# Feed-forward products of an fp32 transformer kernel: one 512-column and one 256-column matmul, or three of 256 columns summed in PSUM

## The chip, the cores and the metric

The kernel runs on one core of a Trainium2 chip. The metric is the device time of one execution in microseconds (us). The program is one launch; weights come from HBM in 314 transfers while the core computes.

## The reference

Two blocks of two layers each act on 256 tokens of width 1024, all in float32. The first block has, per layer, a feed-forward stage, an attention mixer and a second feed-forward stage; the second block has a mixer and a feed-forward stage. There are six feed-forward stages in all, each with an inner width of 2816. What is computed in one (first block; the second block's takes gate and up from one matrix and normalises the result before it is added):

```python
def rms_norm(x, g):
    xf = x.astype(jnp.float32)
    y = xf * lax.rsqrt(jnp.mean(xf * xf, axis=-1, keepdims=True) + RMS_EPS)
    return (y * g.astype(jnp.float32)).astype(x.dtype)

def swiglu(x, w_gate, w_up, w_down):
    return (jax.nn.silu(x @ w_gate) * (x @ w_up)) @ w_down

h = h + 0.5 * swiglu(rms_norm(h, ffn1_norm[l]), ffn1_w_gate[l], ffn1_w_up[l], ffn1_w_down[l])
```

## The kernel before

**Precision.** Every fp32 operand is split in two fp32r halves, a high one (a rounded copy) and a low one (what the copy lost). A product is taken as high x high, high x low and low x high, summed; low x low is left out. Weights and activations both have such halves: `w_hi`, `w_lo` and `x_hl`, `hid_hl`, `m_hl`, where `hl[:, 0, :]` is the high and `hl[:, 1, :]` the low half of 256 tokens, side by side.

**Feed-forward stage.** The activations lie feature by token, so a weight block of 128 x 128 is the stationary operand and the 256 tokens stream past it. `matmul_pair` (line 450) issues two matmuls for a block: one of the high weights with both halves of the activations, 512 columns into a whole PSUM bank (line 452), and one of the low weights with the high half, 256 columns, added into the first half of that bank (line 453). The bank then holds two partial sums of 256 columns, which VectorE (DVE) has yet to add. A stage has 22 gate and up parts in turn (p = 0 to 21, even ones gate, odd ones up; each of 1024 x 256 weights, so 8 x 2 blocks = 16 pairs) and 12 down parts (8, 8 and 6 blocks deep by 2 wide, four times; 176 pairs). That makes 352 + 176 = 528 pairs in a stage and 3168 in six.

**PSUM.** Part p uses two banks, `pair_banks(p)`, in a rotation of three; TensorE (PE) waits before part p until DVE has taken part p - 3. Chunks of the down product have banks of their own (`down_bank`), and banks 6 and 7 are also used for the row statistics.

**DVE in a stage** (`ffn`, line 1221). For each part `both` (line 1231) adds the two halves of two banks in a `tensor_reduce` into SBUF (`g_tmp` or `u_tmp`) and so frees the banks (`up_free`). For a gate part, `scaled_gate` (line 1237) multiplies by `row_b`, the row factor of the normalisation; ScalarE (ACT) applies Silu (line 913). For an up part, `hidden` (line 1242) multiplies gate and up; ACT makes the high half (line 916), and `hidden_lo` (line 1246) the low half. For each down chunk a `tensor_reduce` (line 1277) adds the halves; then lines 1284 and 1285 scale it and add it to `h`, or, in the last stage of each layer of the second block, a second normalisation follows (`post_norm`, line 1179).

**Weights.** A ring of three slots: SyncE's queue loads a part (line 435) once its slot's low half has been made, ACT makes the high half (line 265) once PE has used the part three before, and DVE makes the low half (line 272); PE waits for that.

**The row factor.** In part 0 the squares' sum goes through PE (line 466), DVE (`token_roots`, line 1173), GpSimd (POOL, a power of -0.5, line 1632) and PE again behind part 1 (`to_rows`, line 473); `row_factor` (line 1177) copies it to `row_b`.

**Order.** Each engine's queue is written out by hand and is in order; semaphores tie them. The mixers have their own helpers, `matmul3` (lines 446 to 448, mostly 512 columns) and `project_out`, whose three matmuls (lines 591 to 593) are

```python
nc.tensor.matmul(mixer_out(c), hs[0], mk[:, 0, :], start=first, stop=False, skip_group_check=True)
nc.tensor.matmul(mixer_out(c), hs[0], mk[:, 1, :], start=False, stop=False, skip_group_check=True)
mm = nc.tensor.matmul(mixer_out(c), hs[1], mk[:, 0, :], start=False, stop=m >= 2 and k == kc - 1, skip_group_check=True)
```

Of the kernel before, what the change touches and what calls it, by code (L numbers as in the profile page):

```python
# [17 lines left out]
P = 128  # L18
# [157 lines left out]
def build(nc, w, out):  # L176

    with ExitStack() as ctx:
# [42 lines left out]
        def sem(name):  # L221
            return ctx.enter_context(nc.semaphore(name))
# [11 lines left out]
        up_free, scaled_ready, silu_ready, hid_ready = sem("up_free"), sem("scaled_ready"), sem("silu_ready"), sem("hid_ready")  # L234
# [53 lines left out]
        def pair_banks(p):  # L288

            return 2 * (p % 3)  # L290
# [159 lines left out]
        def matmul_pair(bank, w_h, w_l, hl, start, stop):  # L450

            nc.tensor.matmul(ps[:, bank, :], w_h, hl.rearrange("p x n -> p (x n)"), start=start, stop=False, skip_group_check=True)  # L452
            return nc.tensor.matmul(ps[:, bank, 0:SEQ], w_l, hl[:, 0, :], start=False, stop=stop, skip_group_check=True)  # L453

        @block.tensor
        def _(pe):
# [20 lines left out]
            def ffn(i0, post_norm):  # L477
                x0 = due("xlo_ready", KC) - KC
                u0 = due("up_free", 2 * STEPS) - 2 * STEPS
                h0 = due("hidlo_ready", STEPS) - STEPS  # L480
                for p in range(2 * STEPS):
                    i = i0 + p
                    part_ready(i)
                    if p >= 3:
                        pe.wait_ge(up_free, u0 + p - 2)
# [16 lines left out]
                for q in range(KC // 2):  # L502
                    if q == 1:
                        pe.wait_ge(up_free, u0 + 2 * STEPS)
# [636 lines left out]
        def _(dve):  # L1141
# [79 lines left out]
            def ffn(s, i0, post_norm_):  # L1221
                def both(dst, p):

                    dve.wait_ge(part_used, i0 + p + 1)
                    b = pair_banks(p)
                    taken = STEPS * FFN_BEFORE[s] + p // 2
                    if taken and p % 2 == 0:
                        dve.wait_ge(hid_ready, taken)
                    elif taken:
                        dve.wait_ge(hidlo_ready, taken)  # L1230
                    return nc.vector.tensor_reduce(dst.rearrange("p (f n) -> p f n", f=2), ps[:, b:b + 2, :].rearrange("p b (x n) -> p b n x", x=2),  # L1231
                                                   AX_X, ALU.add).then_inc(up_free, 1)

                def scaled_gate(j):
                    dve.wait_ge(up_free, 2 * STEPS * FFN_BEFORE[s] + 2 * j + 1)
                    g2 = g_tmp.rearrange("p (f n) -> p f n", f=2)
                    nc.vector.tensor_tensor(g2, g2, row_b.unsqueeze(1).to_broadcast([P, 2, SEQ]), ALU.mult).then_inc(scaled_ready, 1)

                def hidden(j):
                    dve.wait_ge(up_free, 2 * STEPS * FFN_BEFORE[s] + 2 * j + 2)  # L1240
                    dve.wait_ge(silu_ready, due("silu_ready"))
                    nc.vector.tensor_tensor(u_tmp, g_tmp, u_tmp, ALU.mult).then_inc(hid_ready, 1)
# [6 lines left out]
                both(g_tmp, 0)  # L1249
# [3 lines left out]
                both(u_tmp, 1)  # L1253
# [4 lines left out]
                for j in range(1, STEPS):  # L1258
                    both(g_tmp, 2 * j)
                    hidden_lo(j - 1)  # L1260
                    scaled_gate(j)
                    split_lo(dve, i0 + 2 * j + 3)
                    both(u_tmp, 2 * j + 1)
                    hidden(j)
                    split_lo(dve, i0 + 2 * j + 4)
                    if s == 0 and j == 1:
                        rope2_angles()
                hidden_lo(STEPS - 1)

                for q in range(KC // 2):  # L1270
                    split_lo(dve, i0 + 2 * STEPS + 3 * q + 3)
                    split_lo(dve, i0 + 2 * STEPS + 3 * q + 4)
                    for c in (2 * q, 2 * q + 1):
# [3 lines left out]
                        m = nc.vector.tensor_reduce(t, ps[:, b, :].rearrange("p (x n) -> p n x", x=2), AX_X, ALU.add)  # L1277
                        if post_norm_:
                            m.then_inc(h_ready, 1)
# [3 lines left out]
                        step(m)  # L1283
                        step(nc.vector.scalar_tensor_tensor(t, t, 0.5, row_b, ALU.mult, ALU.mult))
# [447 lines left out]
```

## Time and profile before

| what | value |
|---|---|
| three runs | 2043.04, 2043.59, 2054.57 us (median 2043.59) |
| the profiled execution | 2051.39 us, span 2049.6 us |
| mean granted TensorE clock | 0.969 of full speed |
| PE busy, DVE busy, ACT busy | 94%, 68%, 46% of the span |
| HBM read | 324 MB, 159 GB/s over the span |

The span runs from the first to the last instruction of the profiled execution; its own time is 1.8 us more. Busy time of PE counts overlapping matmuls once: a matmul's record is longer than the distance to the next one, since the array takes the next matmul before the last has drained. How fast PE goes is therefore read from the distance between starts. PEld is the load of the stationary operand; every matmul has one of its own.

### The profile page before, as it was taken

To read this page: it belongs to the slowest core of one execution; us is meant where nothing else is said; L and a number is where in the kernel's file an instruction comes from. 1 tells how busy PE (TensorE), PEld (TensorE's weight loads), DVE (VectorE), ACT (ScalarE), POOL (GpSimd) and SP (SyncE) were. 2 spreads that over 40 slices of the span, in tenths; PEclk is the share of its full clock that TensorE was granted. 3 is DMA by queue.
4 is the path that set the end of the run, shared out by engine and by line. 5 is a ranking of instruction groups with operands and counts; after the bars stand their busy time and mean duration, and the time that the engine had idled before them with its cause. 6 is when DMAs were issued, how large, how long until landed. Compare 5 with 4: busy or idle time off the path is not lost.

```text
span 2049.6 us, 26068 instructions
## 1 busy us (share of the span) xinstructions
PE 1935.5 (94%) x10928; PEld 1673.8 (82%) x10928; DVE 1394.5 (68%) x1548; ACT 944.3 (46%) x1154; POOL 151.4 (7%) x124
## 2 busy tenths in 40 slices
PE   7999988999999999799999999989997999989997
PEld 6888866988888888679888878878886878878886
DVE  6876678677678776767876446658765446668764
ACT  5444453444444444525444564544443464544442
POOL 0000640000000007200000001100000001100000
PEclk9999998999999999879999999989998999999998
DMA  7555450355555555304545543324554443424552
GB/s 272 185 175 195 164 181 1 124 191 180 184 191 194 180 177 188 134 1 161 189 176 194 185 166 135 128 103 175 188 188 159 144 171 121 157 103 164 191 184 77
DMA packets 47204, 326.77 MB, mean 159 GB/s; under 512 B 5488, under 2 KB 5488, under 8 KB 10864
## 3 DMA queue, kind: packets, MB, share of 16 engines
q1 hardware_dynamic: 46368, 322.78, 44.0%
q10 hardware_dynamic: 720, 2.33, 0.3%
q8 instruction: 86, 1.41, 0.3%
q14 instruction: 30, 0.25, 0.0%
HBM read 324.04 MB, written 1.05 MB: 159 GB/s over the span
## 4 chain that ended last, share of the span: by engine, by line
PE 76%; issue 9%; DVE 7%; POOL 5%; ACT 3%; DMA 0%; POOLq 0%; SPq 0%; ACTq 0%; DVEq 0%
PE ps L452 31%; PE ps L453 16%; PE ps L446 6%; PE ps L448 6%; PE ps L447 6%; ACT w_hi L265 1%; PE ps L644 1%; DVE w_lo L272 1%; POOL arena L1626 1%; PE ps L591 1%; PE ps L593 1%; PE ps L592 1%; POOL arena L1627 1%; POOL arena L1625 1%; PE ps L613 1%
## 5 line engine op out<-in xcount | busy, mean ns | idle before, releaser
L272 DVE TENSOR_TENSOR w_lo<-raw,w_hi 128x2048 fp32r<-128x2048 f32 (+3 forms) x314 | 705.7, 2251 | 334.1 <-ACT w_hi L265 331.7
L265 ACT CAST w_hi<-raw 128x2048 fp32r<-128x2048 f32 (+3 forms) x314 | 583.7, 1861 | 687.6 <-PE ps L453 431.1
L452 PE MATMUL ps<-x_hl,w_hi 128*128 128x512 f32 x2112 | 746.0, 398 | 33.3 <-DVE x_hl L1157 18.1
L453 PE MATMUL ps<-x_hl,w_lo 128*128 128x256 f32 x2112 | 594.8, 282 | 0.0
L452 PEld LDWEIGHTS ps<-x_hl,w_hi 128*128 128x128 f32 x2112 | 399.5, 189 | 125.7 <-issue 33.9
L453 PEld LDWEIGHTS ps<-x_hl,w_lo 128*128 128x128 f32 x2112 | 402.8, 191 | 0.0
L452 PE MATMUL ps<-hid_hl,w_hi 128*128 128x512 f32 x1056 | 371.0, 394 | 0.0
L446 PE MATMUL ps<-w_hi,x_hl 128*128 128x512 f32 (+3 forms) x744 | 287.7, 387 | 15.2 <-DVE x_hl L1157 8.4
L453 PE MATMUL ps<-hid_hl,w_lo 128*128 128x256 f32 x1056 | 299.1, 283 | 0.0
L447 PE MATMUL ps<-w_lo,x_hl 128*128 128x512 f32 (+3 forms) x744 | 283.6, 381 | 0.0
L448 PE MATMUL ps<-w_hi,x_hl 128*128 128x512 f32 (+3 forms) x744 | 283.5, 381 | 0.0
L1231 DVE TENSOR_REDUCE ffn_tmp<-ps 128x512 f32<-128x1024 f32 x132 | 161.6, 1225 | 124.7 <-PE ps L453 124.0
L452 PEld LDWEIGHTS ps<-hid_hl,w_hi 128*128 128x128 f32 x1056 | 198.4, 188 | 45.4
L453 PEld LDWEIGHTS ps<-hid_hl,w_lo 128*128 128x128 f32 x1056 | 198.9, 188 | 0.0
L446 PEld LDWEIGHTS ps<-w_hi,x_hl 128*128 128x128 f32 x744 | 141.6, 190 | 44.3 <-issue 13.8
L448 PEld LDWEIGHTS ps<-w_hi,x_hl 128*128 128x128 f32 x744 | 141.4, 190 | 26.7
L447 PEld LDWEIGHTS ps<-w_lo,x_hl 128*128 128x128 f32 x744 | 141.6, 190 | 25.0
L1632 POOL TENSOR_TENSOR stat<-stat,const 128x2 f32<-128x2 f32 x14 | 19.9, 1423 | 1538.7 <-DVE stat L1173 1029.7
L881 ACT ACTIVATE x_hl<-h,gains 128x256 fp32r<-128x256 f32 x80 | 38.6, 504 | 105.4 <-DVE h L1285 74.5
L591 PE MATMUL ps<-m_hl,w_hi 128*128 128x256 f32 x256 | 73.0, 285 | 0.0
L593 PE MATMUL ps<-m_hl,w_lo 128*128 128x256 f32 x256 | 72.5, 283 | 0.0
L592 PE MATMUL ps<-m_hl,w_hi 128*128 128x256 f32 x256 | 72.5, 283 | 0.0
(215 smaller groups left out, 1704.3 us busy)
## 6 DMA issues: line engine op xcount, KB each, us to landing
raw<-in_parts SPq DMA_DIRECT2D x282, 1024.0 KB, 4.8
raw<-in_parts SPq DMA_DIRECT2D x24, 768.0 KB, 4.2
raw<-in_parts SPq DMA_DIRECT2D x4, 576.0 KB, 3.8
raw<-in_parts SPq DMA_DIRECT2D x2, 832.0 KB, 4.3
raw<-in_parts SPq DMA_DIRECT2D x2, 704.0 KB, 4.0
const<-in_const ACTq DMA_DIRECT2D x1, 1098.0 KB, 8.6
h<-in_x_t SPq DMA_DIRECT2D x2, 512.0 KB, 5.4
out_h<-h SPq DMA_DIRECT2D x4, 256.0 KB, 2.1
```

Of the source, the lines that this page charges most:

```text
L265: nc.scalar.copy(w_hi[:, i % RING, 0:n_of(i)], raw[:, i % RING, 0:n_of(i)]).then_inc(high_ready, 1)
L272: nc.vector.tensor_tensor(w_lo[:, s, 0:n], raw[:, s, 0:n], w_hi[:, s, 0:n].bitcast(F32), ALU.subtract).then_inc(low_ready, 1)
L446: nc.tensor.matmul(out_, a_hi, b_hi, start=start, stop=False, skip_group_check=True)
L447: nc.tensor.matmul(out_, a_hi, b_lo, start=False, stop=False, skip_group_check=True)
L448: return nc.tensor.matmul(out_, a_lo, b_hi, start=False, stop=stop, skip_group_check=True)
L452: nc.tensor.matmul(ps[:, bank, :], w_h, hl.rearrange("p x n -> p (x n)"), start=start, stop=False, skip_group_check=True)
L453: return nc.tensor.matmul(ps[:, bank, 0:SEQ], w_l, hl[:, 0, :], start=False, stop=stop, skip_group_check=True)
L591: nc.tensor.matmul(mixer_out(c), hs[0], mk[:, 0, :], start=first, stop=False, skip_group_check=True)
L592: nc.tensor.matmul(mixer_out(c), hs[0], mk[:, 1, :], start=False, stop=False, skip_group_check=True)
L593: mm = nc.tensor.matmul(mixer_out(c), hs[1], mk[:, 0, :], start=False, stop=m >= 2 and k == kc - 1, skip_group_check=True)
L881: nc.scalar.activation(x_hi(c), h[:, c, :], ACT.Copy, scale=gains[:, s, c:c + 1]).then_inc(xhi_ready, 1)
L1231: return nc.vector.tensor_reduce(dst.rearrange("p (f n) -> p f n", f=2), ps[:, b:b + 2, :].rearrange("p b (x n) -> p b n x", x=2), AX_X, A ...
```

## The change

The 512-column matmul of `matmul_pair` becomes two of 256 columns with the same high weights, first with the high and then with the low half of the activations, and all three matmuls add into the first 256 columns of the bank. The bank then holds the finished sum. The reductions on DVE go: `scaled_gate` and `hidden` read PSUM themselves, and so does the scaling of the down chunks; with the second normalisation a copy of 256 columns stands in the reduction's place. `up_free` goes: PE now waits before part p for `scaled_ready` (p - 3 a gate part) or `hid_ready` (an up part), and before the second pair of down chunks for the last `hid_ready`.

```diff
 def matmul_pair(bank, w_h, w_l, hl, start, stop):
-    nc.tensor.matmul(ps[:, bank, :], w_h, hl.rearrange("p x n -> p (x n)"), start=start, stop=False, skip_group_check=True)
+    nc.tensor.matmul(ps[:, bank, 0:SEQ], w_h, hl[:, 0, :], start=start, stop=False, skip_group_check=True)
+    nc.tensor.matmul(ps[:, bank, 0:SEQ], w_h, hl[:, 1, :], start=False, stop=False, skip_group_check=True)
     return nc.tensor.matmul(ps[:, bank, 0:SEQ], w_l, hl[:, 0, :], start=False, stop=stop, skip_group_check=True)
...
                 if p >= 3:
-                    pe.wait_ge(up_free, u0 + p - 2)
+                    pe.wait_ge(hid_ready if p % 2 == 0 else scaled_ready, u0 + (p - 3) // 2 + 1)
...
                 if q == 1:
-                    pe.wait_ge(up_free, u0 + 2 * STEPS)
+                    pe.wait_ge(hid_ready, u0 + STEPS)
...
             def scaled_gate(j):
-                dve.wait_ge(up_free, 2 * STEPS * FFN_BEFORE[s] + 2 * j + 1)
-                g2 = g_tmp.rearrange("p (f n) -> p f n", f=2)
-                nc.vector.tensor_tensor(g2, g2, row_b.unsqueeze(1).to_broadcast([P, 2, SEQ]), ALU.mult).then_inc(scaled_ready, 1)
+                dve.wait_ge(part_used, i0 + 2 * j + 1)
+                if j or FFN_BEFORE[s]:
+                    dve.wait_ge(hid_ready, STEPS * FFN_BEFORE[s] + j)
+                b = pair_banks(2 * j)
+                nc.vector.tensor_tensor(g_tmp.rearrange("p (f n) -> p f n", f=2), ps[:, b:b + 2, 0:SEQ],
+                                        row_b.unsqueeze(1).to_broadcast([P, 2, SEQ]), ALU.mult).then_inc(scaled_ready, 1)

             def hidden(j):
-                dve.wait_ge(up_free, 2 * STEPS * FFN_BEFORE[s] + 2 * j + 2)
+                dve.wait_ge(part_used, i0 + 2 * j + 2)
                 dve.wait_ge(silu_ready, due("silu_ready"))
-                nc.vector.tensor_tensor(u_tmp, g_tmp, u_tmp, ALU.mult).then_inc(hid_ready, 1)
+                if j or FFN_BEFORE[s]:
+                    dve.wait_ge(hidlo_ready, STEPS * FFN_BEFORE[s] + j)
+                b = pair_banks(2 * j + 1)
+                nc.vector.tensor_tensor(u_tmp.rearrange("p (f n) -> p f n", f=2), ps[:, b:b + 2, 0:SEQ],
+                                        g_tmp.rearrange("p (f n) -> p f n", f=2), ALU.mult).then_inc(hid_ready, 1)
...
-                    m = nc.vector.tensor_reduce(t, ps[:, b, :].rearrange("p (x n) -> p n x", x=2), AX_X, ALU.add)
                     if post_norm_:
-                        m.then_inc(h_ready, 1)
+                        nc.vector.tensor_copy(t, ps[:, b, 0:SEQ]).then_inc(h_ready, 1)
...
-                    step(m)
-                    step(nc.vector.scalar_tensor_tensor(t, t, 0.5, row_b, ALU.mult, ALU.mult))
+                    step(nc.vector.scalar_tensor_tensor(t, ps[:, b, 0:SEQ], 0.5, row_b, ALU.mult, ALU.mult))
```

PE's queue at the start of part 3 of the first stage, the first part that waits for banks; before:

```order
L452 MATMUL ps<-x_hl,w_hi 128x512
L453 MATMUL ps<-x_hl,w_lo 128x256
L452 MATMUL ps<-x_hl,w_hi 128x512 [waits up_free,low_ready]
L453 MATMUL ps<-x_hl,w_lo 128x256
L452 MATMUL ps<-x_hl,w_hi 128x512
```

and with the change:

```order
L452 MATMUL ps<-x_hl,w_hi 128x256
L453 MATMUL ps<-x_hl,w_hi 128x256
L454 MATMUL ps<-x_hl,w_lo 128x256
L452 MATMUL ps<-x_hl,w_hi 128x256 [waits scaled_ready,low_ready]
L453 MATMUL ps<-x_hl,w_hi 128x256
L454 MATMUL ps<-x_hl,w_lo 128x256
```

Two instructions for a block became three, and the wait is now for the scaled gate of part 0.

DVE's queue at the start of the first stage, from the low half of part 2 to the products of parts 0 and 1; before:

```order
L272 TENSOR_TENSOR w_lo<-raw,w_hi 128x2048 [waits high_ready]
L1231 TENSOR_REDUCE ffn_tmp<-ps 128x512 [waits part_used]
L1173 TENSOR_SCALAR stat<-ps 128x2 [waits sum_done]
L272 TENSOR_TENSOR w_lo<-raw,w_hi 128x2048 [waits high_ready]
L1231 TENSOR_REDUCE ffn_tmp<-ps 128x512 [waits part_used]
L1177 COPY arena<-ps 128x256 [waits bcast_done]
L1237 TENSOR_TENSOR ffn_tmp<-ffn_tmp,arena 128x512 [waits up_free,dve_step]
L272 TENSOR_TENSOR w_lo<-raw,w_hi 128x2048 [waits high_ready]
L1242 TENSOR_TENSOR ffn_tmp<-ffn_tmp 128x512 [waits silu_ready,up_free]
```

and with the change (`arena` in the copy and the product is `row_b`):

```order
L272 TENSOR_TENSOR w_lo<-raw,w_hi 128x2048 [waits high_ready]
L1174 TENSOR_SCALAR stat<-ps 128x2 [waits sum_done]
L272 TENSOR_TENSOR w_lo<-raw,w_hi 128x2048 [waits high_ready]
L1178 COPY arena<-ps 128x256 [waits bcast_done]
L1228 TENSOR_TENSOR ffn_tmp<-ps,arena 128x512 [waits part_used,dve_step]
L272 TENSOR_TENSOR w_lo<-raw,w_hi 128x2048 [waits high_ready]
L1237 TENSOR_TENSOR ffn_tmp<-ps,ffn_tmp 128x512 [waits silu_ready,part_used]
```

Both reductions are gone, and the product that frees part 0's banks stands behind the copy of the row factor.

## Rows read from the trace of the kernel before

**Rows 1.** The page, part 1: busy us, share and instructions of each engine.

```profile
PE 1935.5 (94%) x10928; PEld 1673.8 (82%) x10928; DVE 1394.5 (68%) x1548; ACT 944.3 (46%) x1154; POOL 151.4 (7%) x124
```

**Rows 2.** The page, part 4: the chain that ended last, by engine.

```profile
PE 76%; issue 9%; DVE 7%; POOL 5%; ACT 3%; DMA 0%; POOLq 0%; SPq 0%; ACTq 0%; DVEq 0%
```

**Rows 3.** Busy us by engine: last feed-forward stage, then clock; sum of six.

```profile
1848.00:2035.00 187.00, 187.00 (x1063) 164.62 (x1064) 129.60 (x110) 81.60 (x76) 0.69 (x1) 0.99 0.46 163
sum 1116.00, PE 1115.21 PEld 977.69 DVE 821.62 ACT 499.63 POOL 10.38; mean PE 185.87 PEld 162.95 DVE 136.94 ACT 83.27 POOL 1.73
```

**Rows 4.** Line 452 in four stretches: count, ns min/median/max, first and last start.

```profile
L452 PE MATMUL ps<-x_hl,w_hi x320: 393/398/478, 397.6 to 510.4; 128*128 128x512 f32 x160
...
L452 PE MATMUL ps<-x_hl,w_hi x308: 391/394/396, 589.9 to 696.3; 128*128 128x512 f32 x154
...
L452 PE MATMUL ps<-x_hl,w_hi x316: 390/391/392, 1863.9 to 1973.1; 128*128 128x512 f32 x158
...
L452 PE MATMUL ps<-hid_hl,w_hi x176: 386/396/398, 142.6 to 204.1; 128*128 128x512 f32 x176
```

**Rows 5.** Timeline, gate and up products: start us, us, engine, line.

```profile
61.39 0.40 PE L452 MATMUL ps<-x_hl,w_hi 128*128 128x512 f32 x1
61.39 0.19 PEld L453 LDWEIGHTS ps<-x_hl,w_lo 128*128 128x128 f32 x1
61.62 0.28 PE L453 MATMUL ps<-x_hl,w_lo 128*128 128x256 f32 x1
...
61.74 0.40 PE L452 MATMUL ps<-x_hl,w_hi 128*128 128x512 f32 x1
```

**Rows 6.** Timeline, lines 591 to 593 in the first mixer.

```profile
373.26 0.28 PE L591 MATMUL ps<-m_hl,w_hi 128*128 128x256 f32 x1
...
373.38 0.28 PE L592 MATMUL ps<-m_hl,w_hi 128*128 128x256 f32 x1
373.38 0.19 PEld L593 LDWEIGHTS ps<-m_hl,w_lo 128*128 128x128 f32 x1
...
379.02 0.28 PE L591 MATMUL ps<-m_hl,w_hi 128*128 128x256 f32 x1
```

**Rows 7.** Timeline, lines 446 to 448, all of 512 columns.

```profile
1343.66 0.39 PE L446 MATMUL ps<-w_hi,x_hl 128*128 128x512 f32 x1
...
1347.06 0.39 PE L446 MATMUL ps<-w_hi,x_hl 128*128 128x512 f32 x1
```

**Rows 8.** Groups of DVE by form: busy us, mean ns, idle before and releaser.

```profile
L272 DVE TENSOR_TENSOR w_lo<-raw,w_hi 128x2048 fp32r<-128x2048 f32 x282 | 651.2, 2313 | 312.1 <-ACT w_hi L265 309.8
L1231 DVE TENSOR_REDUCE ffn_tmp<-ps 128x512 f32<-128x1024 f32 x132 | 161.6, 1225 | 124.7 <-PE ps L453 124.0
...
L1237 DVE TENSOR_TENSOR ffn_tmp<-ffn_tmp,arena 128x512 f32<-128x512 f32 x66 | 45.3, 686 | 0.2
...
L1277 DVE TENSOR_REDUCE arena<-ps 128x256 f32<-128x512 f32 x48 | 32.5, 684 | 9.2 <-PE ps L453 9.1
...
L1537 DVE TENSOR_TENSOR rows<-rows,arena 128x1024 f32<-128x1024 f32 x8 | 9.8, 1225 | 0.3
L1536 DVE TENSOR_TENSOR arena<-arena,ps 128x1024 f32<-128x1024 f32 x8 | 9.8, 1220 | 9.5 <-PE ps L448 9.5
...
L1177 DVE COPY arena<-ps 128x256 f32<-128x256 f32 x10 | 4.2, 420 | 6.0 <-PE ps L473 6.0
```

**Rows 9.** Timeline, third feed-forward stage, the row factor.

```profile
581.09 1.22 DVE L1231 TENSOR_REDUCE ffn_tmp<-ps 128x512 f32<-128x1024 f32 x1
...
582.45 2.67 POOL L1632 TENSOR_TENSOR stat<-stat,const 128x2 f32<-128x2 f32 x1 [186.13 <-DVE stat L1173]
...
585.18 0.71 PE L473 MATMUL ps<-const,stat 128*128 128x128 f32 x4 [0.79 <-POOL stat L1632]
```

**Rows 10.** Timeline, DVE at the end of the last stage.

```profile
2035.51 0.69 DVE L1277 TENSOR_REDUCE arena<-ps 128x256 f32<-128x512 f32 x1 [1.15 <-PE ps L453]
2036.12 1.33 DVE L1164 TENSOR_TENSOR arena<-arena,rows 128x256 f32<-128x256 f32 x3
```

More of the change, by code:

```diff
@@ L233, in build @@
         gained_ready, sets_clear = sem("gained_ready"), sem("sets_clear")
-        up_free, scaled_ready, silu_ready, hid_ready = sem("up_free"), sem("scaled_ready"), sem("silu_ready"), sem("hid_ready")
+        scaled_ready, silu_ready, hid_ready = sem("scaled_ready"), sem("silu_ready"), sem("hid_ready")
         hidhi_ready, hidlo_ready = sem("hidhi_ready"), sem("hidlo_ready")
@@ L478, in ffn @@
                 x0 = due("xlo_ready", KC) - KC
-                u0 = due("up_free", 2 * STEPS) - 2 * STEPS
+                u0 = due("scaled_ready", STEPS) - STEPS
                 h0 = due("hidlo_ready", STEPS) - STEPS
@@ L1221, in ffn @@
             def ffn(s, i0, post_norm_):
[L1222 to L1232, printed above, removed]
-                def scaled_gate(j):
-                    dve.wait_ge(up_free, 2 * STEPS * FFN_BEFORE[s] + 2 * j + 1)
-                    g2 = g_tmp.rearrange("p (f n) -> p f n", f=2)
-                    nc.vector.tensor_tensor(g2, g2, row_b.unsqueeze(1).to_broadcast([P, 2, SEQ]), ALU.mult).then_inc(scaled_ready, 1)
+                def scaled_gate(j):
+                    dve.wait_ge(part_used, i0 + 2 * j + 1)
[4 more added lines that the diff above has]
+                                            row_b.unsqueeze(1).to_broadcast([P, 2, SEQ]), ALU.mult).then_inc(scaled_ready, 1)
                 def hidden(j):
-                    dve.wait_ge(up_free, 2 * STEPS * FFN_BEFORE[s] + 2 * j + 2)
+                    dve.wait_ge(part_used, i0 + 2 * j + 2)
                     dve.wait_ge(silu_ready, due("silu_ready"))
-                    nc.vector.tensor_tensor(u_tmp, g_tmp, u_tmp, ALU.mult).then_inc(hid_ready, 1)
+                    if j or FFN_BEFORE[s]:
[3 more added lines that the diff above has]
+                                            g_tmp.rearrange("p (f n) -> p f n", f=2), ALU.mult).then_inc(hid_ready, 1)
                 def hidden_lo(j):
@@ L1247, in hidden_lo @@
                                             hid_hl[:, 2 * j:2 * j + 2, 0, :].bitcast(F32), ALU.subtract).then_inc(hidlo_ready, 1)
-                both(g_tmp, 0)
                 token_roots(STATS_FFN)
@@ L1252, in ffn @@
                 split_lo(dve, i0 + 3)
-                both(u_tmp, 1)
                 row_factor(STATS_FFN)
@@ L1258, in ffn @@
                 for j in range(1, STEPS):
-                    both(g_tmp, 2 * j)
                     hidden_lo(j - 1)
@@ L1262, in ffn @@
                     split_lo(dve, i0 + 2 * j + 3)
-                    both(u_tmp, 2 * j + 1)
                     hidden(j)
```

## The prediction

> **What bounds the kernel now.** I read the busy shares first: PE is busy for 94% of the span, DVE for 68%, ACT for 46% [rows 1]. The chain of waits that ended last is PE for 76%, with another 9% of issue time, and DVE only 7% [rows 2]. A share over the whole span mixes mixers and feed-forward stages, and the change touches the latter alone, so next comes the busy time in the six stretches that hold them: 1116 us together, of which PE is busy 1115.2 and DVE 821.6; in the last one PE fills 187.0 of 187.0 us and DVE 129.6, at a granted clock of 0.99 [rows 3]. Inside a feed-forward stage PE waits for next to nothing. What is taken from DVE there is worth nothing unless PE waits for it; what is added to PE is paid in full. So the question is how far a block of weights takes PE on its way, and that is the distance between starts of line 452, not the duration of a record, which overlaps the next.
>
> **The pace of a pair.** Steady gate and up parts: 319 distances in 112.8 us are 353.6 ns a pair in the second stage; 307 in 106.4 us are 346.6 ns in the third; 315 in 109.2 us are 346.7 ns in the last [rows 4]. I read the first stage like the second and the fourth and fifth like the last. Down parts: 175 distances in 61.5 us, 351.4 ns; this row stands for all six stages [rows 4]. Close up, the 512-column matmul takes 0.23 and the 256-column one 0.12 us of such a pair, and each has a weight load of 0.19 us that lies beside the running matmul [rows 5].
>
> **The pace of a triple.** The mixer already has what the change makes: lines 591 to 593 are high x high, high x low and low x high, each of 256 columns, into one region of PSUM. From the first matmul of one triple to the first of the sixteenth after it, 5.76 us pass: 360.0 ns a triple, 120.0 ns a matmul [rows 6]. The second matmul has the weights of the first, and it gets no discount: from 373.26 to 373.38 it is the same 0.12 us [rows 6]. For comparison, fifteen matmuls of 512 columns take 3.40 us, 226.7 ns each [rows 7]. Two points give a line: 106.7 ns more for 256 columns more, which is the rate of the higher of the clock's two levels (2.4 GHz), and 120.0 - 106.7 = 13.3 ns that a matmul costs whatever its width. By that line a pair is 226.7 + 120.0 = 346.7 ns, which is what the last stage shows, and a triple is 360.0. Columns are equal (768 before and after); the one instruction more per block costs the 13.3 ns. Where the pair takes 353.6 or 351.4 ns, something adds 7 or 5 ns to it that no row explains; I assume that it goes with the 512-column form, since the mixer's triple shows no such excess, and take 360.0 everywhere.
>
> The Trainium skill ("TensorE: Matmul & The Clock Gate", section "Wait — 56ns, not 53.3ns?") gives N columns at 2.4 GHz plus about 2.5 ns for back-to-back matmuls; here rows 6 and 7 show 13.3 in place of the 2.5, so the trace does not agree. By the Trainium skill's figure the extra 3168 matmuls would be an estimated 7.9 us, and the sum below +6.3 us.
>
> **The sum, PE.** First and second stage: 2 x 352 x (360.0 - 353.6) = 4.5 us. Third to sixth: 4 x 352 x (360.0 - 346.7) = 18.7 us. Down, six stages: 6 x 176 x (360.0 - 351.4) = 9.1 us. Together 32.3 us on the path.
>
> **The sum, DVE.** 132 reductions of 1225 ns (161.6 us) and 48 of 684 ns go; 16 copies of about 420 ns come for sixteen of the latter [rows 8]. The products now read one operand from PSUM. The same form with and without a PSUM operand, 1024 wide, takes 1220 and 1225 ns, so `scaled_gate` stays at its 686 ns [rows 8]; I price the reads at nothing. The relief is off the path: DVE's largest idle group, 312 us, ends with ACT's high half, which itself waits for PE's use of the slot [rows 8]. Two places give something back. In the third stage the reduction of part 0 stands ahead of the row's mean: 1.22 us on DVE, then 2.67 us on POOL, and PE stood still 0.79 us before the broadcast behind part 1 [rows 9]. With the reduction gone that wait goes: -0.8 us. In the two stages with a second normalisation the last chunk's reduction is on the path (DVE waited for PE before it and the squares follow [rows 10]); a copy instead gives 684 - 420 = 0.26 us, twice where the two last chunks queue up, so -0.8 us for both stages. Between the other stages PE runs on into the next one without a stop, so a shorter chain there gives nothing.
>
> **New waits.** The gate's banks used to be free after a reduction; now they are free after `scaled_gate(0)`, behind the row factor. In the worst stage shown the broadcast ends at 585.18 + 0.71 = 585.9; with 0.42 for the copy and 0.69 for the product the banks are free at 587.0, and PE wants them for part 3 only a whole part (5.76 us) after the broadcast, at 591.6. So 4.6 us of cover; without it each us of lateness would cost up to six. The up banks wait for Silu now, but two parts (11.5 us) lie between the end of part p and part p + 3, against one product of 0.69 us. Both are priced at nothing.
>
> Total: 32.3 - 1.6 = +30.7 us. Against the profiled execution's 2051.4 that is 2082. That execution is 7.8 us above the median of the runs shown (2043.59); the terms are distances within steady stretches, so I put them on the median: **2074 us**. A measurement of this kernel can tell about 1%, 20 us, from no change.
>
> **The rivals.**
> - **A, the added matmul is nearly free.** The price of 13.3 ns would belong to a change of weights or to the long stream of a mixer, and two halves of one operand behind the same weights would pay nothing. For it: the feed-forward pair already runs 5 to 7 ns slower than the line in places, so part of a fixed cost may be paid already. Against it: line 592 follows line 591 with the same weights at 0.12 us [rows 6]. It decides below (20.4 + 1.6) / 3168 = 6.9 ns per block, where the result is within 1%. At 0 ns the time is 2042, not slower than before. Chance 0.13. (The Trainium skill's 2.5 ns, same title and section, would fall under this rival: an estimated 2050.)
> - **B, the excess stays.** What adds 7 and 5 ns in rows 4 is of the stage, not of the form. Then every block gets 13.3 ns: 3168 x 13.3 = 42.1, less 1.6: 2084. The mixer's triple speaks against it. Chance 0.10.
> - **C, a bank comes free late.** If `scaled_gate(0)` is over 4.6 us later than worked out, PE stops before part 3 of every stage; 1 us beyond that is 6 us more, 2080 and up. Or PE can't be fed six instructions per 360 ns over 190 us where it had four per 347; no stretch of this trace shows that pace for more than some 23 us. Chance 0.05, up to about 2095.
> - **D, the stages hung on DVE after all.** If the excess of rows 4 came from DVE's wide PSUM reductions, a lighter DVE gives back 704 x 6.9 + 1056 x 4.7 = 9.8 us beyond the forecast's own assumption at most, and that needs A as well to pass 1%. Chance 0.02.
>
> **How the numbers follow.** The forecast (one triple is 360 ns, give or take 3) has a chance of 0.70; 3 ns are 9.5 us, so its own range is 2064 to 2084. The lowest price that rows allow is zero (A, 2042). The whole range leaves out the lower part of A and the far end of C: 2050 to 2090. Slower by over 1% (beyond 2064): nearly all of the forecast, B and C, 0.81. Within 1%: A and the forecast's low edge, 0.17. Faster by over 1%: 0.02.
>
> **What the profile after would show.** Starts of the three matmuls in a steady part 120 ns apart, and 16 triples in 5.76 us in every stage; if the distances are near 116, A is right, and if the first two stages show over 122, B. PE's busy share in the six stretches near 100%, their sum some 31 us longer. DVE without the two reductions and some 185 us less busy, with PE gaining nothing from it. No wait of PE on the scaled gate or the hidden product before a first matmul of a part; one there of over 1 us is C. The prediction is wrong if the triple is below 356 ns, or if PE waits where it did not.

## The result and the profile after

The changed kernel takes 2074.07 us (median of four runs, 2072.04 to 2074.44), the kernel before 2047.27 us (four runs, the three of the table and one more). The ratio is 1.0118 with a 95% interval of 1.009 to 1.0146: slower by about 24 us (18 to 30), with a direction clear of noise. 2074 was forecast, as 2043.59 and 30.7 more. Executions of the kernel before differ among themselves by up to 12 to 20 us.

The profiled execution took 2072.04 us, its span is 2070.2 us. The page, part 1, answers to [rows 1]:

```profile
PE 1962.0 (95%) x14096; PEld 1835.9 (89%) x14096; DVE 1220.0 (59%) x1384; ACT 930.9 (45%) x1154; POOL 141.2 (7%) x124
```

PE has 3168 matmuls more and is busy 26.5 us longer. DVE has 164 instructions fewer and is busy 174.5 us less. Moving work off DVE did shorten DVE, and the kernel got longer. The six feed-forward stretches, cut as in [rows 3] (bounds, length, busy us of PE, PEld, DVE, ACT and POOL, granted clock, DMA share, GB/s):

```profile
1865.00:2056.00 191.00, 191.00 (x1586) 191.00 (x1585) 102.26 (x86) 78.29 (x73) 0.70 (x1) 0.99 0.46 160
sum 1141.00, PE 1141.00 PEld 1141.00 DVE 650.76 ACT 486.06 POOL 4.19; mean PE 190.17 PEld 190.17 DVE 108.46 ACT 81.01 POOL 0.70
```

PE is busy for all of the 1141.0 us; DVE fell from 821.6 [rows 3] to 650.8 us. Line 452, whose distances from start to start are now those of a triple, in the stretches of [rows 4] (count, shortest, median and longest record in ns, first and last start in us):

```profile
L452 PE MATMUL ps<-x_hl,w_hi x319: 283/283/363, 400.2 to 514.8; 128*128 128x256 f32 x160
...
L452 PE MATMUL ps<-x_hl,w_hi x304: 282/283/283, 590.9 to 700.0; 128*128 128x256 f32 x152
...
L452 PE MATMUL ps<-x_hl,w_hi x315: 283/283/283, 1879.8 to 1992.8; 128*128 128x256 f32 x158
...
L452 PE MATMUL ps<-hid_hl,w_hi x176: 279/281/285, 144.2 to 206.5; 128*128 128x256 f32 x176
```

318 distances in 114.6 us are 360.4 ns, with the end of the row factor's broadcast in it; 303 in 109.1 us are 360.1; 314 in 113.0 us are 359.9. Down parts: 175 in 62.3 us, 356.0 ns. Close up, each matmul starts 0.12 us after the last, those of the same weights (452 to 453) like those of new ones:

```profile
61.65 0.28 PE L454 MATMUL ps<-x_hl,w_lo 128*128 128x256 f32 x1
61.77 0.28 PE L452 MATMUL ps<-x_hl,w_hi 128*128 128x256 f32 x1
61.89 0.28 PE L453 MATMUL ps<-x_hl,w_hi 128*128 128x256 f32 x1
62.01 0.28 PE L454 MATMUL ps<-x_hl,w_lo 128*128 128x256 f32 x1
62.13 0.28 PE L452 MATMUL ps<-x_hl,w_hi 128*128 128x256 f32 x1
62.25 0.28 PE L453 MATMUL ps<-x_hl,w_hi 128*128 128x256 f32 x1
```

What a whole stage takes, by the first and last start of line 452: the gate and up parts of the first stage (its down parts stand in [rows 4] and above), and the whole last stage. Before, and then after:

```profile
L452 PE MATMUL ps<-x_hl,w_hi x352: 391/398/764, 15.2 to 142.3; 128*128 128x512 f32 x176
...
L452 PE MATMUL ps<-x_hl,w_hi x352: 390/391/767, 1847.9 to 1973.1; 128*128 128x512 f32 x176
L452 PE MATMUL ps<-hid_hl,w_hi x176: 386/396/400, 1973.5 to 2034.9; 128*128 128x512 f32 x176
```

```profile
L452 PE MATMUL ps<-x_hl,w_hi x352: 280/283/550, 14.7 to 143.8; 128*128 128x256 f32 x176
...
L452 PE MATMUL ps<-x_hl,w_hi x352: 278/283/551, 1864.1 to 1993.5; 128*128 128x256 f32 x176
L452 PE MATMUL ps<-hid_hl,w_hi x176: 279/281/285, 1993.9 to 2056.2; 128*128 128x256 f32 x176
```

The first stage went from 188.9 to 191.8 us, the last from 187.0 to 192.1. Summed in this way, the six stages went from 1119.5 to 1146.3 us: +26.9. The two spans differ by 20.6 only, because the rest of this profile of the kernel before was long; a second profile of it (below) settles that.

### The profile page after: what moved, and what is told of

It reads as the page before. It is cut to its first block, busy times and chain, and to the rows that moved or that the text cites. A ratio compares the mean times of both kernels' runs of the same rounds, so it can differ in the third digit from the quotient of the medians.

```text
span 2070.2 us, 32170 instructions
## 1 busy us (share of the span) xinstructions
PE 1962.0 (95%) x14096; PEld 1835.9 (89%) x14096; DVE 1220.0 (59%) x1384; ACT 930.9 (45%) x1154; POOL 141.2 (7%) x124
## 4 chain that ended last, share of the span: by engine, by line
PE 76%; issue 9%; DVE 7%; POOL 4%; ACT 3%; DMA 0%; POOLq 0%; SPq 0%; ACTq 0%; DVEq 0%
PE ps L452 16%; PE ps L453 16%; PE ps L454 16%; PE ps L446 6%; PE ps L448 6%; PE ps L447 6%; ACT w_hi L265 1%; DVE w_lo L272 1%; POOL arena L1616 1%; PE ps L592 1%; PE ps L594 1%; PE ps L593 1%; POOL arena L1617 1%; PE ps L645 1%; POOL arena L1615 1%
## 5 line engine op out<-in xcount | busy, mean ns | idle before, releaser
L452 PE MATMUL ps<-x_hl,w_hi 128*128 128x256 f32 x2112 | 602.4, 285 | 32.8 <-DVE x_hl L1158 18.1
L453 PE MATMUL ps<-x_hl,w_hi 128*128 128x256 f32 x2112 | 600.6, 284 | 0.0
L452 PEld LDWEIGHTS ps<-x_hl,w_hi 128*128 128x128 f32 x2112 | 408.7, 194 | 33.5 <-issue 33.5
L453 PEld LDWEIGHTS ps<-x_hl,w_hi 128*128 128x128 f32 x2112 | 408.8, 194 | 0.0
L454 PEld LDWEIGHTS ps<-x_hl,w_lo 128*128 128x128 f32 x2112 | 408.5, 193 | 0.0
L453 PE MATMUL ps<-hid_hl,w_hi 128*128 128x256 f32 x1056 | 297.2, 281 | 0.0
L452 PE MATMUL ps<-hid_hl,w_hi 128*128 128x256 f32 x1056 | 297.2, 281 | 0.0
L452 PEld LDWEIGHTS ps<-hid_hl,w_hi 128*128 128x128 f32 x1056 | 198.8, 188 | 0.0
L453 PEld LDWEIGHTS ps<-hid_hl,w_hi 128*128 128x128 f32 x1056 | 198.8, 188 | 0.0
L446 PEld LDWEIGHTS ps<-w_hi,x_hl 128*128 128x128 f32 x744 | 141.6, 190 | 44.3 <-issue 13.9
L1622 POOL TENSOR_TENSOR stat<-stat,const 128x2 f32<-128x2 f32 x14 | 9.8, 699 | 1559.9 <-DVE stat L1174 1043.5
L1237 DVE TENSOR_TENSOR ffn_tmp<-ps,ffn_tmp 128x512 f32<-128x512 f32 x66 | 45.6, 691 | 79.1 <-PE ps L454 79.1
```

The costliest lines, as they stand in the source:

```text
L446: nc.tensor.matmul(out_, a_hi, b_hi, start=start, stop=False, skip_group_check=True)
L452: nc.tensor.matmul(ps[:, bank, 0:SEQ], w_h, hl[:, 0, :], start=start, stop=False, skip_group_check=True)
L453: nc.tensor.matmul(ps[:, bank, 0:SEQ], w_h, hl[:, 1, :], start=False, stop=False, skip_group_check=True)
L1237: nc.vector.tensor_tensor(u_tmp.rearrange("p (f n) -> p f n", f=2), ps[:, b:b + 2, 0:SEQ], g_tmp.rearrange("p (f n) -> p f n", f=2), ALU.m ...
```

## The experiments

**The split alone.** The kernel before, and only line 452 cut in two; reductions and waits stay.

```diff
-nc.tensor.matmul(ps[:, bank, :], w_h, hl.rearrange("p x n -> p (x n)"), start=start, stop=False, skip_group_check=True)
+nc.tensor.matmul(ps[:, bank, 0:SEQ], w_h, hl[:, 0, :], start=start, stop=False, skip_group_check=True)
+nc.tensor.matmul(ps[:, bank, SEQ:2 * SEQ], w_h, hl[:, 1, :], start=False, stop=False, skip_group_check=True)
```

> The kernel before, with the 512-column matmul split into two of 256 columns that write the two halves of the bank; the reductions on DVE and all waits stay. Theory (a matmul costs 13.3 ns besides its columns, wherever it writes, and DVE's relief is worth nothing): three matmuls of 120 ns a block in gate and up parts, 16 blocks in 5.76 us, PE 27 us longer over the six feed-forward stages, time 26 to 32 us above the kernel before, 0 to 4 above the changed kernel. Rival (the cost of the change lies in adding three times into the same 256 columns of PSUM): this one stays within 8 us of the kernel before. Rival (DVE's relief had hidden part of a larger cost): this one is over 8 us slower than the changed kernel.

Measured: 2071.6 us (four runs, 2068.72 to 2073.09) against 2049.44 of the kernel before in the same comparison (13 runs, 2041.97 to 2061.75): 1.0097, interval 1.0064 to 1.0129. The pace is that of the changed kernel:

```profile
L452 PE MATMUL ps<-x_hl,w_hi x279: 282/283/284, 599.8 to 699.8; 128*128 128x256 f32 x140
```

278 distances in 100.0 us: 359.7 ns. The cost of the change is in the instruction that it adds to each block; adding up in the same columns costs nothing that shows, and with all the DVE work that the change removes this kernel is no slower than the changed one (2071.6 and 2074.07 us).

**The DVE side alone.** The changed kernel with the old pair on PE:

```diff
-nc.tensor.matmul(ps[:, bank, 0:SEQ], w_h, hl[:, 0, :], start=start, stop=False, skip_group_check=True)
-nc.tensor.matmul(ps[:, bank, 0:SEQ], w_h, hl[:, 1, :], start=False, stop=False, skip_group_check=True)
+nc.tensor.matmul(ps[:, bank, :], w_h, hl.rearrange("p x n -> p (x n)"), start=start, stop=False, skip_group_check=True)
```

> The changed kernel with the pair of the kernel before in place of the three matmuls. DVE reads the first half of the bank only, so the high x low product is computed but left out of the sum. This is the DVE side of the change alone. Theory: PE does what it did before, so the time is that of the kernel before less 1 to 3 us (row factor of the third stage, last chunks of two stages). Rival (DVE's wide reductions slow PE in the first two stages and the down parts, 353.6 and 351.4 ns a pair): these become 347, and the time is 8 to 12 us below the kernel before. Rival (the new waits on the scaled gate and the hidden product cost something): slower than the kernel before.

Measured: 2044.03 us (ten runs, 2035.6 to 2053.7), 0.9972, interval 0.9945 to 0.9998. So 132 wide reductions and 32 narrower ones fewer, and the rest of the change's DVE side, give 0.3%, some 6 us with an interval from 0 to 11. Forecast were 1 to 3 us. More than that is not shown to come from DVE: from the first to the last matmul of each, the six stages of this profile take 1125.8 us together, those of the kernel before 1120.8, and the runs here had a higher granted clock (0.973 in the mean, against 0.971), which goes with a shorter time, as the next experiment shows. The new waits cost nothing that shows. The rival of a lighter DVE that speeds PE up falls: from the second stage on, every gate and up pair is at the slower pace, and the down parts are at 351.4 ns as before.

```profile
L452 PE MATMUL ps<-x_hl,w_hi x310: 395/398/403, 394.6 to 503.8; 128*128 128x512 f32 x155
...
L452 PE MATMUL ps<-x_hl,w_hi x284: 395/398/403, 589.7 to 689.7; 128*128 128x512 f32 x142
```

309 distances in 109.2 us are 353.4 ns, 283 in 100.0 us likewise.

**The kernel before, a second profile.** No edit.

> The kernel before, a second profile of it. If the slower pairs of the first two stages and of the down parts (353.6 and 351.4 ns) belong to the program, they are at the same places. If they are the state of the chip in one execution, the pace is 347 or another one elsewhere. The stretches outside the feed-forward stages, 6 us shorter in the changed kernel's profile, show how much they differ between two executions of one program.

Measured: 2043.88 us. The second stage, 346.7 ns a pair ((504.7 - 394.8) / 317), and the third, 353.4 ((689.9 - 589.9) / 283):

```profile
L452 PE MATMUL ps<-x_hl,w_hi x318: 391/391/396, 394.8 to 504.7; 128*128 128x512 f32 x159
...
L452 PE MATMUL ps<-x_hl,w_hi x284: 395/398/403, 589.9 to 689.9; 128*128 128x512 f32 x142
```

In the first profile it was the other way round, 353.6 in the second and 346.6 in the third [rows 4]. The pair has two paces, and a stage takes one of them in its first parts and keeps it: here stages 1, 2 and 4 were fast, in the first profile stages 3 to 6. The down parts are at 351.4 ns in both. Outside the stages the first profile spent 930.1 us, this one 921.7 and the changed kernel's 923.9: the 6 us by which the changed kernel seemed shorter there were the first profile's own.

So the two paces are not what sets these two executions of one program apart: summed by line 452, the stages take 1119.5 us in the first and 1120.4 in this one, and the other 8 us lie outside. There the granted clock differs. The stretch between the fourth and the fifth stage, in the first profile and in this one (bounds, length, busy us of PE, PEld, DVE, ACT and POOL, granted clock, DMA share, GB/s):

```profile
1126.00:1387.00 261.00, 243.19 (x1324) 207.07 (x1322) 145.18 (x158) 130.32 (x187) 17.86 (x24) 0.96 0.39 141
```

```profile
1118.00:1374.00 256.00, 237.51 (x1322) 201.93 (x1320) 144.82 (x159) 130.48 (x187) 17.85 (x24) 0.98 0.40 143
```

The same work takes 261 us at a mean clock of 0.96 and 256 at 0.98. Over the whole span the means are 0.969 and 0.971; with full speed and half of it as the only levels (2.4 and 1.2 GHz) that is an estimated 128 and 117 us at the lower one. The run times follow it: of 22 runs of the kernel before (those that the grouping below is compared with) the three with a mean clock of 0.966 to 0.968 took 2058.7 to 2059.7 us, the three with 0.974 or 0.975 took 2041.6 to 2046.4. A straight line through the 22 falls by some 1.7 us for each 0.001 of the clock. A slow pace in a stage can't do that, since it makes a stretch at full clock longer and so raises the mean. What keeps the clock low for longer in one execution than in another, no run shows.

**Order within a block.** The changed kernel, its last two matmuls exchanged, so that equal weights never follow each other within a block.

```diff
-nc.tensor.matmul(ps[:, bank, 0:SEQ], w_h, hl[:, 1, :], start=False, stop=False, skip_group_check=True)
-return nc.tensor.matmul(ps[:, bank, 0:SEQ], w_l, hl[:, 0, :], start=False, stop=stop, skip_group_check=True)
+nc.tensor.matmul(ps[:, bank, 0:SEQ], w_l, hl[:, 0, :], start=False, stop=False, skip_group_check=True)
+return nc.tensor.matmul(ps[:, bank, 0:SEQ], w_h, hl[:, 1, :], start=False, stop=stop, skip_group_check=True)
```

> The changed kernel with the last two matmuls of a block exchanged: high weights, low weights, high weights again, so that within a block no two matmuls in a row have the same stationary operand. Theory (each matmul loads its own operand beside the one before, same or not): 120 ns each, the time of the changed kernel within 5 us. Rival (a repeated operand is cheaper to load): each block gets longer, by up to 13 ns, 40 us in all.

Measured: 2072.0 us in one run, and 278 distances in 100.1 us, 360.1 ns. A repeated operand gets no discount.

```profile
L452 PE MATMUL ps<-x_hl,w_hi x279: 283/283/283, 599.9 to 700.0; 128*128 128x256 f32 x140
```

**Narrower still.** As many instructions and columns as the changed kernel, cut at 384 instead of 256; reductions stay.

```diff
-nc.tensor.matmul(ps[:, bank, :], w_h, hl.rearrange("p x n -> p (x n)"), start=start, stop=False, skip_group_check=True)
+flat = hl.rearrange("p x n -> p (x n)")
+nc.tensor.matmul(ps[:, bank, 0:384], w_h, flat[:, 0:384], start=start, stop=False, skip_group_check=True)
+nc.tensor.matmul(ps[:, bank, 384:512], w_h, flat[:, 384:512], start=False, stop=False, skip_group_check=True)
```

> The kernel before with its 512-column matmul split into 384 and 128 columns, each into its part of the bank; reductions stay. As many instructions and columns as the changed kernel. Theory of a fixed 13.3 ns beside the columns, alone: 173 + 67 + 120 = 360 ns a block, time as the changed kernel. Theory with a floor under a narrow matmul (matmuls of 208 and 176 columns start 110 ns apart in the kernel before, where the line says 100 and 87): the 128-column one takes 110 or more, 403 ns a block, 43 ns x 3168 = 136 us above the changed kernel, near 2210 us.

Measured: 2224.17 us in one run, 150 above the changed kernel; 222 distances in 90.3 us are 406.8 ns a block. The timeline shows where it goes (start, length, engine, line):

```profile
L453 PE MATMUL ps<-x_hl,w_hi x223: 336/338/346, 649.7 to 740.0; 128*128 128x384 f32 x112
```

```profile
659.87 0.34 PE L453 MATMUL ps<-x_hl,w_hi 128*128 128x384 f32 x1
660.05 0.22 PE L454 MATMUL ps<-x_hl,w_hi 128*128 128x128 f32 x1
660.11 0.33 PE L455 MATMUL ps<-x_hl,w_lo 128*128 128x256 f32 x1
660.28 0.35 PE L453 MATMUL ps<-x_hl,w_hi 128*128 128x384 f32 x1
```

After the 384-column matmul the next starts at 0.18 us, after the 128-column one at 0.06; but the 256-column matmul behind it takes until 0.17 instead of 0.12. Its own record is longer as well, 0.33 us instead of 0.28. 47 ns are lost per block, near the 43 that the expectation's floor gave. The natural reading is that the 128 columns pass too quickly to cover the load of the following matmul's weights. For it: in this trace as in those of the kernel before and of the changed one, no two consecutive loads of `w_hi` or `w_lo` start less than 0.105 us apart, and behind the 128-column matmul the next starts after 0.06. But no run changed the load alone, so this is argued and not shown. Either way, with fp32r operands 256 columns is about as narrow as this kernel can go at 13 ns an instruction: the mixers' matmuls of 208 columns already start 110 ns apart in the kernel before, where the line gives 100.

**Where relief of DVE would count.** Two kernels leave high x low out of the feed-forward products, so that PE needs two matmuls of 256 columns per block. One is the changed kernel with

```diff
-nc.tensor.matmul(ps[:, bank, 0:SEQ], w_h, hl[:, 1, :], start=False, stop=False, skip_group_check=True)
```

> The changed kernel without its second matmul: high x low is left out in the feed-forward stages. PE is a third shorter there: 2 x 120 = 240 ns a block, 3.84 us a part. DVE needs 2 x 2.29 + 2 x 0.69 + 0.68 = 6.6 us for two parts, less than 7.7, ACT 5.1. Theory (each matmul is paid in full): 3168 x 120 = 380 us less than the changed kernel, near 1694 us. Rival (another engine or the weight transfers, 1 MB per 3.84 us or 273 GB/s, become the bound): above 1720 us, with waits of PE on the low half of the weights.

The other is the kernel before with

```diff
-nc.tensor.matmul(ps[:, bank, :], w_h, hl.rearrange("p x n -> p (x n)"), start=start, stop=False, skip_group_check=True)
-return nc.tensor.matmul(ps[:, bank, 0:SEQ], w_l, hl[:, 0, :], start=False, stop=stop, skip_group_check=True)
+nc.tensor.matmul(ps[:, bank, 0:SEQ], w_h, hl[:, 0, :], start=start, stop=False, skip_group_check=True)
+return nc.tensor.matmul(ps[:, bank, SEQ:2 * SEQ], w_l, hl[:, 0, :], start=False, stop=stop, skip_group_check=True)
```

> The kernel before with two matmuls of 256 columns per block: high x high into the first half of the bank, low x high into the second; high x low is left out, and DVE's reductions stay. PE as in the run with two matmuls and no reductions, 7.7 us for two parts; DVE 6.6 + 2 x 1.23 = 9.1 us for two parts. Theory (relief of DVE is worth nothing only as long as PE is slower): here DVE is the bound, 1.4 us for each of 66 double parts, 60 to 95 us slower than its partner without reductions, near 1775 us. Rival (reductions still hide): within 10 us of its partner.

Measured: without reductions 1705.31 us (two runs), with them 1793.74 (two runs), 88 us apart. In a stretch of the third stage, without and then with reductions (bounds, length, busy us of PE, PEld, DVE, ACT, POOL, clock, DMA share, GB/s):

```profile
480.00:560.00 80.00, 80.00 (x671) 80.00 (x670) 65.97 (x57) 50.26 (x44) 0.00 (x0) 1.00 0.78 281
```

```profile
520.00:600.00 80.00, 75.94 (x602) 72.76 (x601) 79.36 (x64) 45.23 (x37) 0.00 (x0) 1.00 0.69 244
```

In the first PE fills the stretch and DVE has 14 us left of 80; in the second DVE is busy 79.4 of 80 us and PE is not. Who waited for whom, PE's first rows of the second kernel (engine, line, waited for: us in total, times, longest):

```profile
PE ps L452 <- DVE w_lo L272: 55.6, 64, 14.8
```

64 waits for the low half of the weights; its partner without reductions has three (17.5 us), the kernel before one (15.2 us, at the very start). The same reductions that were worth next to nothing cost 88 us once PE is a third faster. Of these, the six stages from first to last matmul show 76 (858.8 against 782.4 us). The other 11 lie outside the stages, where nothing was edited and the clock was low for longer (mean over the span 0.961 against 0.968). The 369 us that the first of the two gains over the changed kernel are 3168 x 116 ns, 11 us short of the 380 expected: at 3.84 us a part the starts of the stages are no longer covered (for POOL's row factor PE waits 6.5 us in six places instead of 2.1 in two, for the low half 17.5 us instead of 14.7).

**Two attempts at a single pace.** Grouping: in each output block the wide matmuls first, then the narrow ones.

```diff
+def wide_then_narrow(bank, blocks):
+    for w_h, w_l, hl, start, stop in blocks:
+        nc.tensor.matmul(ps[:, bank, :], w_h, hl.rearrange("p x n -> p (x n)"), start=start, stop=False, skip_group_check=True)
+    for w_h, w_l, hl, start, stop in blocks:
+        m = nc.tensor.matmul(ps[:, bank, 0:SEQ], w_l, hl[:, 0, :], start=False, stop=stop, skip_group_check=True)
+    return m
```

> The kernel before with its 512-column matmuls of one output block issued first, then its 256-column ones (8 and 8 in gate, up and most down parts; the first part and the first down chunk, whose operands arrive one by one, keep the pairs). Same instructions, columns and DVE work. Theory (the 353.6 ns that a pair takes in some stages, in one execution here and in the next there, and its 351.4 ns in down parts come from wide and narrow matmuls taking turns): every block at 226.7 + 120.0 = 346.7 ns or a little less, 3 to 12 us below the kernel before and with a smaller spread. Rival (the excess is the stage's, whatever the order): same time as the kernel before, within 3 us.

Measured: 2043.83 us (twelve runs, 2036.23 to 2048.23) against 2051.14 of the kernel before in the same comparison (22 runs, 2041.58 to 2059.7): 0.9962, interval 0.9944 to 0.998. The pace is one and the same in all six stages, but it is not 346.7:

```profile
L458 PE MATMUL ps<-x_hl,w_hi x303: 389/390/398, 589.8 to 694.5; 128*128 128x512 f32 x152
```

```profile
430.78 2.00 PE L458 MATMUL ps<-x_hl,w_hi 128*128 128x512 f32 x8
432.62 1.11 PE L460 MATMUL ps<-x_hl,w_lo 128*128 128x256 f32 x8
433.57 0.63 PE L458 MATMUL ps<-x_hl,w_hi 128*128 128x512 f32 x2
```

Eight wide ones take 1.84 us (230 ns each), eight narrow ones 0.95 (119), 349 ns a block. That ends the slow pace and gives up the fast one. In the down parts grouping changes nothing (351.7 ns a block, 351.4 before), so their excess does not come from wide and narrow matmuls taking turns.

Where the 7 us come from is not shown. From the first to the last matmul of each, the six stages take 1120.8 us here, and 1120.8 and 1121.8 in the two profiles of the kernel before, with two and three stages at the slow pace. Part goes with the clock (mean of the runs 0.973, against 0.971). At equal clock, by a straight line fitted to the runs of both kernels together, some 5 us are left (an estimate, give or take 2). Exchanging the two matmuls of a pair keeps both paces:

```diff
-nc.tensor.matmul(ps[:, bank, :], w_h, hl.rearrange("p x n -> p (x n)"), start=start, stop=False, skip_group_check=True)
-return nc.tensor.matmul(ps[:, bank, 0:SEQ], w_l, hl[:, 0, :], start=False, stop=stop, skip_group_check=True)
+nc.tensor.matmul(ps[:, bank, 0:SEQ], w_l, hl[:, 0, :], start=start, stop=False, skip_group_check=True)
+return nc.tensor.matmul(ps[:, bank, :], w_h, hl.rearrange("p x n -> p (x n)"), start=False, stop=stop, skip_group_check=True)
```

> The kernel before with the two matmuls of a pair exchanged, the 256-column one first. Theory (turns of wide and narrow matmuls can fall into one of two paces, whichever comes first): each stage at either 346.7 or 353.6 ns a pair, time between 2036 and 2062 us. Rival (the order within a pair decides): one pace in all stages.

Measured: 2031.74 us in one run. Its second stage ran at 346.7 ns ((499.7 - 395.0) / 302), its third at 353.4 ((687.7 - 589.8) / 277); five of the six stages were fast. That is worth some 4 us over the first profile of the kernel before (1116.5 against 1120.8 us in the stages, from first to last matmul); the stretches outside give 15 more (913 against 929 us), at a mean granted clock of 0.978 against 0.969. One run is no verdict.

```profile
L452 PE MATMUL ps<-x_hl,w_lo x303: 280/280/280, 395.0 to 499.7; 128*128 128x256 f32 x152
...
L452 PE MATMUL ps<-x_hl,w_lo x278: 277/281/284, 589.8 to 687.7; 128*128 128x256 f32 x139
```

**The mean ahead of the reduction.** In `ffn` on DVE, with the grouping and then without it:

```diff
-both(g_tmp, 0)
 token_roots(STATS_FFN)
 due("root_ready")
+both(g_tmp, 0)
```

> The same grouping, and the row's mean taken on DVE ahead of the reduction of part 0. Theory (in the kernel before POOL's power took 2.7 us where it started within 0.2 us of a low-half subtraction on DVE, and PE waited for it in one stage): POOL takes 0.7 us in all stages, PE's wait of 0.8 us behind part 1 of the third stage goes, so 0 to 2 us below the run with the grouping alone. Rival (that wait was the only one and covered elsewhere): no difference.

Measured: 2040.49 us (eleven runs, 2038.62 to 2043.13), 0.9949, interval 0.9931 to 0.9967, the best version of this study: some 10 us (0.5%) below the kernel before and 34 below the changed one's 2074.07, and it leaves nothing out. PE's wait for the power in the third stage is gone (POOL made PE wait 2.1 us in all instead of 2.9). Against the grouping alone it is 3.3 us faster, where 0 to 2 were expected; but the stages of the two profiles differ by 0.5 us only (1120.3 and 1120.8), the clock was 0.975 in the mean against 0.973, and at equal clock, estimated as above, both are the same 5 us below the kernel before.

> The kernel before with the row's mean taken on DVE ahead of the reduction of part 0, and the pairs as they were. Theory (the gain of the best run so far is mostly the one pace that grouping gives): this one is within 2 us of the kernel before, still spread over some 15 us, each stage at 346.9 or 353.6 ns a pair. Rival (the early mean is the gain): 5 us or more below the kernel before.

Measured: 2051.74 us (twelve runs, 2038.98 to 2062.24), 1.0009, interval 0.9989 to 1.0029. Alone it gives nothing and leaves the spread; in its profile the first and the last stage were at the fast pace and the four in between at the slow one. So the gain comes with the grouping. The narrow spread does not: the grouping alone spreads over 12 us, both edits together over 4.5, and no run shows why.

## Why the prediction was right

**The bound.** PE fills the feed-forward stages and DVE does not: shown, from both sides. The split alone costs 1.0097, the DVE side alone gives 0.9972, with no gain in the stages of its profile. DVE is busy 174.5 us less, not some 185: its 164 instructions fewer each overlapped the next by some 0.08 us, as at 2036.12 in [rows 10], and busy time counts that once.

**The pace of a triple.** 120.0 ns a matmul read off the mixer's lines 591 to 593 [rows 6] is what the new lines 452 to 454 do, in the gate and up parts of all stages. Rival A (the added matmul is nearly free) falls with it: 452 to 453 is no shorter than 453 to 454, and the run with the other order takes the same. The columns-plus-13.3-ns line holds at 256 and 512 columns; at 128 it fails (406.8 instead of 360 ns).

**The excess.** That the 7 ns by which some stages exceed the line belong to the 512-column form was assumed, and holds: neither the changed kernel nor the split alone shows them, and the lighter DVE does not remove them, so rivals B and D fall. What was not seen is that they change from execution to execution. The sum took two slow stages and four fast ones from one profile; with all six fast the gate and up term is 6 x 352 x 13.3 = 28.1 us, with all six slow 6 x 352 x 6.6 = 13.9 us, and 23.2 was taken. So the paces alone can move the kernel before by 14 us. But the five profiles with the old pair (two of the kernel before, the DVE side alone, the exchanged pair and the early mean) have one to five slow stages, which is 9 us, and their times don't follow that number (2045.3 us with five slow stages, 2051.4 with two) but the granted clock. The changed kernel has one pace, and its four runs spread over 2.4 us; their mean clock was also 0.970 in every one of them, so how much of that calm the single pace gives is open.

**The down term was too large.** Forecast 9.1 us, at 360.0 ns; the triple takes 356.0 there, so 6 x 176 x 4.6 = 4.9 us. "16 triples in 5.76 us in every stage" thus holds for the gate and up parts alone, and in the down parts the triple stands at the very limit (356 ns) below which the prediction called itself wrong. Why the same instructions are 4 ns faster when the tokens that stream past are `hid_hl`'s, while the pair is 4 to 5 ns slower there than at its fast pace, stays open: the starts cycle through 115 to 122 ns, and no run here varied the place of the buffers.

**The sum.** 4.5 + 18.7 + 4.9 = 28.1, less 0.8 for the row factor, is 27.3; the stages show 26.9.

**The gains.** The wait behind part 1 of the third stage is gone. At the end of the last stage a copy of 0.42 us stands where the reduction took 0.69 [rows 10], as worked out; no run isolates what the two stages gained by it:

```profile
2056.81 0.42 DVE L1270 COPY arena<-ps 128x256 f32<-128x256 f32 x1 [1.45 <-PE ps L454]
```

**The base.** The total was put on a median of three runs, 2043.59; with more runs the kernel before has 2047 to 2051. So the difference came out as 23 to 27 us, and the 30.7 forecast lay just beyond the interval of 18 to 30. That the time of 2074 was met to 0.1 us is luck: a down term 4 us too large and a base 4 us or more too low cancelled. The mechanism and its main term were right.

**The new waits.** Rival C did not come. PE waits in the stages for what it waited for before; the whole list for line 452, after:

```profile
PE ps L452 <- DVE x_hl L1158: 18.1, 4, 8.4
...
PE ps L452 <- DVE w_lo L272: 14.7, 1, 14.7
```

Both are stage starts, as in the kernel before (18.1 and 15.2 us). In the third stage the product that frees part 0's banks ran at 591.19 to 591.88 us, with part 3 due one part (5.83 us) after 590.45, at 596.3: 4.4 us of cover, where 4.6 had been worked out.

```profile
590.09 0.60 PE L474 MATMUL ps<-const,stat 128*128 128x128 f32 x4
...
590.73 0.42 DVE L1178 COPY arena<-ps 128x256 f32<-128x256 f32 x1 [2.36 <-PE ps L474]
...
591.19 0.69 DVE L1228 TENSOR_TENSOR ffn_tmp<-ps,arena 128x512 f32<-128x512 f32 x1
```

## What to carry to other kernels

Splitting one matmul into two of the same columns is not free on an engine that is full: each instruction has a part that does not shrink with its columns (13.3 ns here), and it is set against what the other engine's relief is worth, which is next to nothing while that engine has time to spare (and some 80 us here once it has none). Look for the new form elsewhere in the same kernel, since its distance between starts is the price. Before putting a predicted difference on a median, look whether the kernel has a spread of its own, and in what: here a steady stretch read in one profile was one of two paces, and the granted clock of the stretches that the change does not touch moved the total by more. A difference of a few us between two versions should be read in the changed stages, or with the clock of the runs beside it.

## What the runs showed that was not expected

- A turn of 512 and 256 columns runs at 346.7 or 353.4 ns, a stage at a time, in the same program; three matmuls of 256 run at 360.0 in every gate and up stretch, and eight wide ones before eight narrow at 349. Down parts run at 356.0 and 351.7, and the pair there at 351 in every profile.
- Most of the spread of one program over its runs goes with the mean granted clock (0.966 to 0.975 over 22 runs, 18 us), and not with the two paces.
- A 128-column matmul delays the one behind it by some 47 ns.
- POOL's power of two elements took 0.70 us, but 2.67 to 2.85 us in five of 14 places of the kernel before, where a low-half subtraction on DVE had just begun or began with it, as POOL's row at 582.45 in [rows 9] behind DVE's:

```profile
582.29 2.28 DVE L272 TENSOR_TENSOR w_lo<-raw,w_hi 128x2048 fp32r<-128x2048 f32 x1
```

With the reductions gone DVE asks for that subtraction too early for ACT, starts it later, and POOL is through in 0.70 us in all 14 places:

```profile
L1632 POOL TENSOR_TENSOR stat<-stat,const x14: 695/706/2851, 24.8 to 2039.1; 128x2 f32<-128x2 f32 x14
```

```profile
L1622 POOL TENSOR_TENSOR stat<-stat,const x14: 695/696/707, 23.2 to 2059.7; 128x2 f32<-128x2 f32 x14
```

It was covered in all but one place, so it gave back 0.8 us and not 10.

By the Trainium skill ("SBUF — State Buffer", section "Who interferes with whom") a DVE instruction with two inputs in SBUF contends with a GpSimd one that reads SBUF, and the one issued first holds the port; the trace agrees, with 2.67 us behind a subtraction of 2.28 us and 0.70 us ahead of one. The reverse case does not show: a subtraction that began 0.55 us after POOL's start (at 24.78 us) still took 2.29 us.
